# Start addresses of the SBUF tiles: multiples of 64 bytes, and two groups at multiples of 2048

## The reference

```
x = x + concat(gmlp_gating(gelu(h Wu), gelu(h Wv)), memory_attention(h Wq, mem)) @ a_w_out   # layer a
x = x + (silu(conv(h W_gate)) * conv(h W_up)) @ a_ffn_out                                    # D_FF = 2816
k, v, f = rmsnorm(x) @ w_kv
x = x + concat(forgetting_attention(q, k, v, cumsum(log_sigmoid(f))), memory_attention(..)) @ b_w_out
x = x + conv_ffn(x)                                                                          # layer b
x = rmsnorm(x)
# second block: adaptive norm, 8 stick-breaking heads, 4 differential heads, gates, w_out_2
x = x + gate * (concat(stick_breaking * silu(g), rmsnorm(diff_attention) * silu(g)) @ w_out_2)
```

## Time and profile before

| | us |
|---|---|
| median of 3 runs | 1594.12 |
| lowest and highest of them | 1592.28, 1594.25 |
| the profiled execution, its own time | 1589.25 |
| span of its trace | 1587.4 |
| TensorE matmul busy | 1510.7 (95% of the span) |
| VectorE, ScalarE, GpSimd busy | 931.4, 671.4, 110.5 |

### The profile page before, as it was taken

How to read it: one execution, slowest core, us unless ns; L and a number is a source line. 1 busy time by engine, 2 the same in 40 slices (tenths; PEclk the granted TensorE clock), 3 DMA queues, 4 the chain that set the end, 5 groups by cost and what they waited for, 6 DMA issues and landing times.

```text
span 1587.4 us, 20131 instructions
## 1 busy us (share of the span) xinstructions
PE 1510.7 (95%) x7120; PEld 1169.9 (74%) x7120; DVE 931.4 (59%) x1361; ACT 671.4 (42%) x1083; POOL 110.5 (7%) x127
## 2 busy tenths in 40 slices
PE   5988999999999999999989999999999799999998
PEld 4866677888888887766668888888887466667767
DVE  6668667777774335645445777777343644445662
ACT  6533344444443223434344444444222345555561
POOL 1269300000000000000000000000000010000000
PEclk9999999999999999999999999999999899999999
DMA  6544122223223222111112223223322111111221
GB/s 230 178 166 172 41 80 90 96 94 102 95 97 109 92 86 80 54 54 54 49 44 94 93 94 105 92 92 112 104 92 76 62 54 53 55 64 56 67 93 53
DMA packets 38146, 141.85 MB, mean 89 GB/s; under 512 B 4356, under 2 KB 4612, under 8 KB 38088
## 3 DMA queue, kind: packets, MB, share of 16 engines
q1 hardware_dynamic: 36936, 138.98, 25.8%
q10 hardware_dynamic: 1152, 2.10, 0.3%
HBM read 138.97 MB, written 2.10 MB: 89 GB/s over the span
## 4 chain that ended last, share of the span: by engine, by line
PE 83%; DVE 8%; ACT 5%; issue 2%; POOL 1%; DMA 1%; SPq 0%; ACTq 0%; DVEq 0%
PE ps L329 17%; PE ps L330 17%; PE ps L331 17%; PE ps L345 7%; PE ps L347 6%; PE ps L346 6%; DVE wl L263 2%; PE ps L510 2%; PE ps L580 1%; DVE rbc L426 1%; ACT wh L257 1%; PE ps L568 1%; PE ps L1796 1%; POOL aw L800 1%; PE ps L1786 1%
## 5 line engine op out<-in xcount | busy, mean ns | idle before, releaser
L257 ACT CAST wh<-raw 128x1024 fp32r<-128x1024 f32 (+1 forms) x213 | 234.0, 1099 | 312.1 <-PE ps L331 259.3
L263 DVE TENSOR_TENSOR wl<-raw,wh 128x1024 fp32r<-128x1024 f32 (+1 forms) x213 | 275.3, 1292 | 134.9 <-ACT wh L257 134.6
L329 PE MATMUL ps<-xh,wh 128*128 128x512 f32 x728 | 286.0, 393 | 9.7 <-DVE xl L1402 8.0
L330 PE MATMUL ps<-xl,wh 128*128 128x512 f32 x728 | 284.0, 390 | 0.0
L331 PE MATMUL ps<-xh,wl 128*128 128x512 f32 x728 | 283.9, 390 | 0.0
L345 PE MATMUL ps<-xh,wh 128*128 128x512 f32 x448 | 193.0, 431 | 2.5 <-DVE wl L263 2.5
L347 PE MATMUL ps<-xh,wl 128*128 128x512 f32 x448 | 177.8, 397 | 0.0
L346 PE MATMUL ps<-xl,wh 128*128 128x512 f32 x448 | 177.2, 396 | 0.0
L329 PEld LDWEIGHTS ps<-xh,wh 128*128 128x128 f32 x728 | 136.9, 188 | 43.6 <-issue 8.6
L331 PEld LDWEIGHTS ps<-xh,wl 128*128 128x128 f32 x728 | 137.1, 188 | 28.8
L330 PEld LDWEIGHTS ps<-xl,wh 128*128 128x128 f32 x728 | 137.1, 188 | 28.4 <-issue 0.5
(11 more groups left out here) (264 smaller groups left out, 2178.2 us busy)
## 6 DMA issues: line engine op xcount, KB each, us to landing
raw<-w_a_f SPq DMA_DIRECT2D x44, 512.0 KB, 3.2
raw<-w_b_f SPq DMA_DIRECT2D x44, 512.0 KB, 3.2
aw<-w_ada SPq DMA_DIRECT2D x24, 512.0 KB, 5.3
raw<-w_a_f SPq DMA_DIRECT2D x16, 704.0 KB, 4.1
raw<-w_b_f SPq DMA_DIRECT2D x16, 704.0 KB, 4.1
raw<-w_b_pair SPq DMA_DIRECT2D x18, 512.0 KB, 3.2
raw<-w_sb SPq DMA_DIRECT2D x16, 512.0 KB, 3.2
raw<-w_df SPq DMA_DIRECT2D x16, 512.0 KB, 3.2
```

Source lines behind the costliest of these rows:

```text
L257: nc.scalar.copy(wh[:, s, :width], raw[:, s, :width]).then_inc(w_hi, 1)
L263: nc.vector.tensor_tensor(wl[:, s, :width], raw[:, s, :width], wh[:, s, :width].bitcast(F32), ALU.subtract).then_inc(w_lo, 1)
L329: nc.tensor.matmul(dst, a, h(k), start=(k == 0), stop=False)
L330: nc.tensor.matmul(dst, a, l(k), start=False, stop=False)
```

## The change

`next_byte` starts at `nc.sbuf_base` and is rounded to 64 bytes in place of 32 after every tile. Before `xt`, and again before the shared region at `A`, it is rounded up to a multiple of 2048. Nothing else is touched: same tiles, same sizes, same instructions in the same order.

```diff
+LINE, PAGE = 64, 2048
...
-        next_byte = [(nc.sbuf_base + 31) // 32 * 32]
+        next_byte = [nc.sbuf_base]
+
+        def align(n):
+
+            next_byte[0] = (next_byte[0] + n - 1) // n * n
+
+        align(LINE)
...
             if at is None:
                 at = next_byte[0]
-                next_byte[0] += (n + 31) // 32 * 32
+                next_byte[0] += n
+                align(LINE)
             return nc.alloc_sbuf_tensor_at(name, shape, dt, offset=at)
...
         kb = sb("kb", [P, NB16], BF16)
+        align(PAGE)
         xt = sb("xt", [P, KD, S], F32)
...
         wst = sb("wst", [P, 4, P], F32, ct_at + 2048)
+        align(PAGE)
         A, KB = next_byte[0], 1024
```

## The result

The changed kernel takes 1581.84 us (median of 6 runs, 1579.19 to 1585.72) where the kernel before takes 1592.18 (6 runs): a ratio of 0.9941, 95% interval 0.9926 to 0.9957. The profiled execution's span is 1577.4 us, 10.0 less than before.

What follows compares the result with a forecast made beforehand. TensorE's start-to-start matmul distance was taken as the bound. Gains of 11.2 (shared-region streams), 0.2 (memory projections) and 0.1 (VectorE, ScalarE) sum to 11.5 us, from 1594.1 to 1582.6 us; likeliest range 1579.5 to 1585, 8 in 10 1572 to 1595.

Steps and rivals of the forecast that it cites:

- The reading of the trace: TensorE's 512-column matmuls start 226.7 ns apart streaming `xh` in `a_f1`, 233.3 ns streaming `hth` in `a_f2` or `mixh` in `a_out`.
- The unbroken runs: 1500 matmuls streaming the shared region in `f2` stages, `a_out`, `b_out`, `b_qm` and the `c_out` tail would gain 10.0 us.
- The groups between attention steps: The other 324 matmuls streaming the shared region, in small groups, would gain between 0 and 2.2 us, taken as 1.2.
- The mechanism of the 6.67 ns: In shared-region streams, a 2048-byte row starting 32 bytes off touches 33 pieces of 64 bytes, not 32, costing 16 cycles.
- The memory projections: 192 matmuls of 256 columns, `memha` to `memlb`, would gain about 3.3 ns each, 0 to 0.6 us, taken as 0.2.
- The place: Rival: upper SBUF or how those stages are issued makes the 233.3 ns, so nothing changes; time 1594, chance 0.12.
- More than 64 bytes matter: Rival: wider alignment also speeds `xh` streams, one more 16-cycle step for 5352 matmuls; 1547 us, chance 0.11.
- Equal remainders collide: Rival: tiles equal modulo 2048 make TensorE's reads meet VectorE's and ScalarE's in `a_f1`, `b_f1`; 23.5 us slower, 1606, chance 0.04.
- the rule of 16-byte cachelines: Skill's rule for SBUF: tiles at multiples of 32 already hold whole lines, so no gain; its chance was weighed with the rivals.
- VectorE, ScalarE, DMA and the plain float32 matmuls: VectorE and ScalarE would gain 0.1 us, DMA 0 within half a microsecond either way, plain float32 attention matmuls 0.

## Why the prediction was right, point by point

*The reading of the trace.* There are two step lengths, 226.7 and 233.3 ns, in stretches where nothing but TensorE bounds the time: this held, and so did the size. The slow groups in unbroken runs did move to 226.7 ns, neither more nor less. That the place of the streaming tile alone sets the step did not hold; why it looked so follows below.

*The unbroken runs, 10.0 us.* Measured: `a_f2` and `b_f2` 3.52 + 3.51 (7.04 were reckoned), `a_out` and `b_out` 0.94 + 0.92 (1.92), the tail of `c_out` 0.67 (0.72), `b_qm` nothing (0.32 were reckoned: its first job gained 0.14 us, but the second waits for VectorE and started 8.74 us behind the stage's first matmul in both kernels, and a stretch at half clock follows in both). Together 9.56 us of the 10.0. Elsewhere nothing took TensorE's place, as said.

*The groups between attention steps, 1.2 us.* Measured 0.1 at most: the term is within its bounds of 0 to 2.2 and at their lower end. The stage before `a_out` kept 22.3 us, the early `c_out` blocks 26.1, and `b_pair` had gained 0.1 us when the half clock set in. `b_pair` took 201.9 us in the experiment with `xh` off and 202.1 with all weights off, against 201.8 before: the distance is worth next to nothing there. The 1.44 us that `b_pair` got longer are the stretch at half clock, which the prediction had not priced. In the traces of the experiments `b_pair` took 203.1 to 205.4 us nine times, in slow kernels and fast ones, and 201.9 to 202.1 three times. Whether the shorter stages bring the half clock about stays open.

*The mechanism of the 6.67 ns failed.* The step was "A row of 2048 bytes then touches 33 pieces of 64 bytes in place of 32". It gave the right number by luck: the 6.67 ns came from the trace, and the changed kernel puts moving tiles and weights alike at 0 modulo 256, which meets the real condition together with the supposed one. Before, `xh` and the weights both stood at 384 modulo 512, at distance 0, and the shared region at distance 224; so the fast tiles were the ones that agreed with the weights, and not the ones on the 64-byte grid. With all operands off the 64-byte grid by 32 the gain is whole; with moving rows on the grid and weights off it is gone; with both on the grid at a distance of 64, 96, 128 or 192 it is partly or wholly gone. What stands in its place is the distance between TensorE's two reads, the moving row and the weight block. That these meet in the same part of the memory is likely, since a weight block is loaded while the matmul before it streams its rows (in the trace with `wl` off a load of 188 ns starts 2 ns behind the matmul at 345.13 us, and ends before the next), but it is argued, not shown.

*The memory projections, 0.2 us.* The sign was wrong: some 3.3 ns less for each matmul were reckoned. After the change the 256-column matmuls step by 120.0 ns (41.34 to 46.02 us, 39 steps) where they did by 118.2; the experiments with distances of 64 and 224 have 117.8 and 118.3 there, that with everything off by 32 has 120.0. For half the columns distance 0 is the slower one, by at most 0.3 us for all 192 (an estimate from the two steps).

```profile
41.34 0.28 PE L341 MATMUL ps<-memhb,wl 128*128 128x256 f32 x1
...
46.02 0.28 PE L341 MATMUL ps<-memhb,wl 128*128 128x256 f32 x1
```

The 1.85 us gained up to the end of that stage are no part of the mechanism: over the traces of the twelve experiments the first matmul starts between 10.2 and 11.05 us and the stage lasts 37.5 to 40.2, in no order of alignment; the changed kernel taken again had 40.1 where it had 38.1. The 10.0 us between the two traces add up as 9.56 + 1.85 - 1.44 = 9.97 us, where this luck and the half clock in `b_pair` nearly cancel. The gain forecast was 11.5 us; the medians of six runs each give 10.3. The time forecast, 1582.6 us, came within 0.8 of 1581.84 because the kernel before, too, measured lower with six runs, 1592.18 and not 1594.12.

*The rivals.* The place is refuted: `A` went from 133216 to 135168, still the upper part, and the step fell. "More than 64 bytes matter" was right in its title and wrong in its yield: the period is 256, but `xh` was at distance 0 already, so there was nothing more to get. "Equal remainders collide" is refuted for the engines among each other (`a_f1` kept its 241.39 us), and turned round for TensorE's own operands: equal remainders are the best case for 512 columns. By the rule of 16-byte cachelines that the prediction took from the Trainium skill's "SBUF — State Buffer", section "Door 1: The DMA port swizzle", there would have been no gain; ten us were measured. The same page of the Trainium skill, in "Who interferes with whom", gives TensorE two independent SBUF read ports, one for the moving operand and one for the weights. The runs here don't agree in full: moving `wl` alone by 32 bytes, and nothing of the moving operand, lengthened the steps in `a_f1` from 226.7 to 233.3 ns.

*VectorE, ScalarE, DMA and the plain float32 matmuls.* As said: the add of `hid` 692 ns (693), that into `acc` 690 (690), chunks of `a_f1` landing in 3.2 us as before. The float32 logits lasted 272/481/693 ns again in the second block, and in layer b 272/482/737, the longest at the half clock. By the addresses, `kr` stood at distance 224 from its weights `qr` before and `kts` at 0 from `qts`, with the same durations: in plain float32 no effect of the distance is seen in them.

A correction to the labels of the earlier trace rows: `a_f2` begins at 483.87 us, so the stretch from 300 to 500 has 16 us of it, and that from 540 to 610 ends in `gate`. The steps of the earlier trace rows, which carried the sum, are from inside their stages.

## What to carry to other kernels

When two groups of matmuls of one shape show two step lengths at full clock, compare the addresses of both operands, not of one. For streams of 512 columns of fp32r with a new 128x128 weight block for each matmul, the only kind shown here, allot the moving tiles and all the weight tiles so that their start addresses are equal modulo 256, with row and block pitches that keep it so; it is worth up to 3% of such a stretch (226.7 ns in place of 233.3) and costs some bytes. A round number that works is not yet its reason: moving each operand by itself, and then both, showed in three kernels what the first success hid.

## What the runs showed that was not expected

The step as a function of the distance is neither monotonic nor the same for every width: best at 0 and second at 64 for 512 columns, while 256 columns are 2.2 ns faster at 64 and 1.7 at 224 than at 0. Only at distance 0 are all steps of 512 columns alike (226 or 227 ns); elsewhere the mean hides a repeating pattern, such as 226, 229, 232 ns at 64, 231 and 235 in turn at 224, and at 128 and 384 either 238 and 229 in turn or seven steps between 228 and 241. `mixh` at 384 showed the one pattern in `a_out` and the other in `b_out`, at the same addresses, so the distance alone does not fix the step. That a step depends on those before it is the likely reason; no run isolates it. With different distances for `wh` and `wl` (the run with `wl` off) even the pairs at distance 0 lengthened. At half clock none of it shows: 213 to 214 ns for 256 columns at any distance. Where the distance changes from row to row (the pitch of 2112 bytes) the pattern came back after 512 bytes, not 256, for which the same reason is likely and not shown either. Why 13.3 ns beyond the columns' own 213.3 remain at distance 0 is open.
